# Sink attention: the low part of a weight tile is made one unit later, and the scalar engine's copies out of PSUM are moved ahead of the high part

## The reference, cut to what matters

```python
def attention_mixer(h, norm_w, w_in, q_norm_w, k_norm_w, sinks, w_out):
    u = rms_norm(h, norm_w) @ w_in
    q, k, v, gate = jnp.split(u, [...], axis=-1)
    q = rms_norm(q..., q_norm_w); k = rms_norm(k..., k_norm_w)
    o = banded_sink_attention(q, k, v, sinks)   # softmax over band, meta tokens and sink
    return (o * jax.nn.silu(gate)) @ w_out
```

## Time and profile before

| | us |
|---|---|
| times of three runs | 1647.33, 1652.02, 1652.57 |
| median | 1652.02 |
| span of the profiled execution, first to last instruction (no time of its own beside it) | 1649.1 |
| sink attention, first score matmul to first output matmul | 1150.7 to 1222.1 |
| TensorE busy | 1598.4 (97%) |
| VectorE busy | 1166.7 (71%) |
| ScalarE busy | 907.0 (55%) |
| DMA traffic | 230.02 MB, mean 139 GB/s |

### The profile page before, as it was taken

How to read it: one execution, slowest core, us unless ns; L and a number is a source line. 1 busy time by engine, 2 the same in 40 slices (tenths; PEclk the granted TensorE clock), 3 DMA queues, 4 the chain that set the end, 5 groups by cost and what they waited for, 6 DMA issues and landing times. The chain is left out here.

```text
span 1649.1 us, 33817 instructions
## 1 busy us (share of the span) xinstructions
PE 1598.4 (97%) x12970; PEld 1430.6 (87%) x12970; DVE 1166.7 (71%) x2011; ACT 907.0 (55%) x1622; POOL 74.0 (4%) x41
## 2 busy tenths in 40 slices
PE   7999999999999999999999999999899999999998
PEld 6888988999999999998888888887667889888877
DVE  5678666789888999986666666655765657655565
ACT  4347653454555767766666666653665644344443
POOL 0000000200000000000000000000001333200000
PEclk9989999999999999999999999999999999999999
DMA  6542355565554444446666666643123445300014
GB/s 225 189 134 86 117 158 167 166 183 169 184 178 144 140 139 131 139 140 207 191 192 192 192 196 194 191 134 103 52 77 93 151 152 155 122 10 3 3 35 145
DMA packets 63222, 230.02 MB, mean 139 GB/s; under 512 B 7024, under 2 KB 7280, under 8 KB 63104
## 3 DMA queue, kind: packets, MB, share of 16 engines
q1 hardware_dynamic: 63104, 228.37, 44.6%
HBM read 227.30 MB, written 1.05 MB: 138 GB/s over the span
## 5 line engine op out<-in xcount | busy, mean ns | idle before, releaser
L1141 DVE TENSOR_TENSOR tile_low<-weights,tile_high 128x1024 fp32r<-128x1024 f32 x252 | 307.9, 1222 | 141.3 <-ACT tile_high L1131 141.1
L1131 ACT ACTIVATE tile_high<-weights 128x1024 fp32r<-128x1024 f32 x252 | 268.1, 1064 | 134.0 <-issue 134.0
L183 ACT ACTIVATE tile_high<-weights 128x1024 fp32r<-128x1024 f32 x169 | 178.4, 1058 | 236.4 <-issue 61.9
L1213 PE MATMUL banks<-parts,tile_high 128*128 128x256 f32 x2048 | 272.0, 286 | 0.9 <-ACT tile_high L1131 0.6
L195 DVE TENSOR_TENSOR tile_low<-weights,tile_high 128x1024 fp32r<-128x1024 f32 x146 | 179.8, 1233 | 130.7 <-ACT tile_high L183 115.7
L1213 PEld LDWEIGHTS banks<-parts,tile_high 128*128 128x128 f32 x2048 | 255.5, 193 | 1.7 <-issue 1.7
L1533 PE MATMUL banks<-tile_high,parts 128*128 128x512 f32 x1024 | 253.0, 389 | 0.9 <-ACT parts L1491 0.9
L1533 PEld LDWEIGHTS banks<-tile_high,parts 128*128 128x128 f32 x1024 | 192.2, 188 | 40.9 <-issue 1.1
L237 PE MATMUL banks<-parts,tile_high 128*128 128x272 f32 (+1 forms) x1216 | 169.5, 293 | 0.0
L237 PEld LDWEIGHTS banks<-parts,tile_high 128*128 128x128 f32 x1216 | 158.1, 192 | 8.7 <-issue 7.5
L1218 PE MATMUL banks<-parts,tile_low 128*128 128x256 f32 x1024 | 144.3, 284 | 4.1 <-DVE tile_low L1141 4.0
(11 more groups left out here) (402 smaller groups left out, 2163.1 us busy)
## 6 DMA issues: line engine op xcount, KB each, us to landing
weights<-in_peer_u SPq DMA_DIRECT2D x128, 512.0 KB, 3.5
weights<-in_peer_v SPq DMA_DIRECT2D x128, 512.0 KB, 3.5
weights<-in_dn_in SPq DMA_DIRECT2D x49, 512.0 KB, 3.5
weights<-in_in_t SPq DMA_DIRECT2D x19, 512.0 KB, 3.6
weights<-in_attn_t SPq DMA_DIRECT2D x19, 512.0 KB, 3.6
weights<-in_in_m SPq DMA_DIRECT2D x16, 512.0 KB, 3.6
weights<-in_wq SPq DMA_DIRECT2D x16, 512.0 KB, 4.2
weights<-in_dn_out SPq DMA_DIRECT2D x16, 512.0 KB, 3.6
```

What stands on the lines that cost most here:

```text
L183: k.nc.scalar.activation(k.high[:, m % 2, :], k.ring.view(n), ACT.Copy).then_inc(*k.high_made.up())
L1131: k.nc.scalar.activation(k.high[:, (s + j) % 2, :], k.ring.buf[:, j % RING, :], ACT.Copy).then_inc(k.high_made.sem, 1)
L1141: k.nc.vector.tensor_tensor(k.low[:, (s + j) % 2, :], k.ring.buf[:, j % RING, :], k.high[:, (s + j) % 2, :].bitcast(F32), ALU.subtract).th ...
L1213: ins = nc.tensor.matmul(ps[:, bank, 0:S], high[:, c, :], x[:, c, :], start=part + c == 0, stop=False)
```

## The change

On DVE, `make_low` for the tile of an even unit moves from the end of that unit to the end of the next (odd) one. On ACT, `store` and `copy_turned` move ahead of `make_high` (and of `open_gates(0)` in the last turn) and of the gate copy. The amount of work is the same.

```diff
                 if u in meta_steps:
                     meta["vector"][meta_steps.index(u)](dve)
-                if u in ahead:
-                    make_low(dve, k, ahead[u])
+                if u - 1 in ahead:
+                    make_low(dve, k, ahead[u - 1])
...
                 if u < len(units):
                     exps(u)
+                if u >= 2:
+                    store(u - 2)
+                if 1 <= u <= len(units):
+                    copy_turned(u - 1)
                 if u == len(units):
                     open_gates(0)
                 elif u in ahead:
                     make_high(act, k, ahead[u])
                 if u and u % 2 == 0:
                     act.wait_ge(k.ring.used.sem, gate_tile(u // 2 - 1) + 1)
                     nc.scalar.activation(T[:, GATE + u // 2 - 1, :], fill, ACT.Copy).then_inc(*gated.up())
-                if u >= 2:
-                    store(u - 2)
-                if 1 <= u <= len(units):
-                    copy_turned(u - 1)
```

## The result

The changed kernel took 1669.02 us (median of 4 runs, 1665.58 to 1673.06) against 1651.04 us for the kernel before (4 runs), a ratio of 1.0115 with a 95% interval of 1.0098 to 1.0132. It is slower by 18 us. The forecast was 1665, from 1657.5 to 1671. The profiled execution of the changed kernel took 1665.58 us, with a span of 1663.8.

What follows compares the result with a forecast made beforehand. PE was taken as the bound, busy 63.29 of 71.37 us. Net stalls +7.0, last turn +1.9 and clock drops +4.2 gave +13.1 us on the 1652.0 median: 1665 us, range 1657.5 to 1671.

Steps and rivals of the forecast that it cites:

- `make_low` later removes the old gaps and costs nothing elsewhere: DVE's list: PE's waits for scale before turn, 4.6 us in seven units, can go; later low parts cost 0.
- The gate copy's stall: ACT's list, even units 2 to 14: PE waits 1.72 us for the late gate copy, 12.0 us in all.
- Old gaps vanish after the stall, net +7.0: PE in units 2 to 14: 5.0 us of old gaps go against 12.0 of stalls, net +7.0 us.
- The last turn, +1.9: Stage end: open_gates(0) behind copy_turned(15) puts the first output matmul 5.33 us after turn(15), not 3.46, +1.9 us.
- The clock, three drops of 1.4 = 4.2 us: PE's clock after the seven stalls: three falls to 0.50 at 1.4 us, 4.2 us; bounds 0 and 9.8.
- The count, two to five: PE's clock in the stage: two to five new stretches at 0.50; this forecast case had chance 0.55.
- the drop at the stage's end: First output matmuls: PE's clock falls to 0.50 there before and after, so no added cost was counted.
- nearly every stall: Rival, PE's clock: six or seven drops add 8.4 to 9.8 us, 1669 to 1671 us; chance 0.12.
- Mostly hidden: Rival: DVE sets the pace, each stall costs only 0.6 us, 4.2 in all, so 1656 us; chance 0.07.
- faster: Rival: part 1 saves 4.6 us, the ACT copies moved ahead cost nothing, 1647 us; chance 0.04.
- Clock stays up: Rival, PE's clock: at most one drop in seven gaps, +8.9 to 10.3, 1661 to 1662 us; chance 0.22.

Runs made afterwards that it cites:

- the last experiment: Kernel before with make_low one unit later, plus 4 filling matmuls ahead of values(15): 1644.81 us, ratio 0.9980.
- The stalls filled: Changed kernel plus 7 idle matmuls on PE in each of the seven gate-copy stalls: 1663.33 us, ratio 1.0088.
- DVE edit alone: Kernel before with only make_low moved to the odd unit, ACT's list as before: 1645.08 us, ratio 0.9976.
- the filled kernel: Changed kernel plus 7 idle matmuls per stall, 4 ahead of values(15) and 10 behind it: 1661.16 us, ratio 1.0073.
- the first execution: First profiled execution of the changed kernel, nothing further changed: 1665.58 us, turn 1 to 15 in 71.25 us.
- the second execution: Another profiled execution of the changed kernel, nothing further changed: turn 1 to 15 in 76.84 us.

## Why the prediction was right or wrong

- **`make_low` later removes the old gaps and costs nothing elsewhere: right.** Alone it made the kernel 4 us faster. Turn 1 to 15 fell from 59.13 to 55.53 us, although one step there (5-6, 5.14) holds a drop of the clock, and to 54.15 in the execution of the last experiment, which holds none; 4.6 us of gaps were forecast.
- **The gate copy's stall: right, mechanism and size.** Forecast 7 x 1.72 = 12.0 us, measured 11.8. The single stalls were 1.67 in four units, 1.33 and 1.45 in units 6 and 8, where the longer scores of tt = 1 already run ahead of the short copy of tt = 0, and 2.32 in unit 14. That one I had missed: no scores are left there to cover its first 0.66 us. The misses cancel but for 0.2 us, which is luck. That the gate copy's place is the cause is shown by putting it first: no stall, no loss.
- **Old gaps vanish after the stall, net +7.0: right.** The stalls filled, less one drop, gave +7.1.
- **The last turn, +1.9: right.** The output was forecast 5.33 us after `turn(15)` and came after 5.48, which is +2.0 on the 3.46 of the kernel before, and restoring only that turn took it back (to 2.86). The price is larger than it looks: the 3.46 hold values matmuls at the lower clock (1.53 us, 1.02 at full). At the full clock the same turn takes 2.96 (DVE edit alone) or 2.86, so the late Silu costs 2.5 to 2.6 us of waiting there. In the changed kernel the Silu starts 1.29 us after its table load, which is now exposed. The page "ScalarE: Activation LUTs" of the Trainium skill, section "What ACT_TABLE_LOAD costs", counts a drain of some 1.38 us on top. The trace doesn't show one: the load begins 0.02 us after the copy ahead of it ends (1231.97), so the measured step holds.
- **The clock, three drops of 1.4 = 4.2 us: too small.** This is the term that failed in size. The waits make 9.1 us of the 18 to 21 that the change cost, and the clock's part is 9 us by the filled kernel, more where that one kept a drop. The count, two to five, was right: three drops in the stage in the first execution, five in the second. Their price was not. Beyond the 66.2 us that turn 1 to 15 takes with the stalls alone, three drops cost 71.25 - 66.2 = 5.1 us and five cost 10.6, so 1.7 to 2.1 each. I had priced a drop by the one group of matmuls after it, but there are long stretches at the lower clock (0.57 mean over 12 us and twice over 8 us in the second execution) through which PE works on. And I wrote that the drop at the stage's end is there before and after: it is longer after, 5.02 and 5.28 us for the first output group against 3.96. Two gaps (1.09 and 2.54 us) stand there where one stood, but they don't settle it alone, since behind the same two gaps the group took 4.50 us with the gate copy put first. One of the drops, in unit 5 to 6, comes without any stall too. Without one it costs 1.5 us (5.14 against 3.64 us in an execution that holds no drop), with the stall 2.2 in the first execution and 3.7 in the second, over steps 5-6 and 6-7.
- **The forecast as a whole: the sum was 4.9 us short, the level 4.0.** Forecast +13.1, measured +18.0; the base of 1652.0 was 1 us above the kernel before as it was measured beside the changed one, and that hides a part of the miss. The median lies in the upper half of the range, where only the rival "nearly every stall" (1669 to 1671) stood. That rival had the time but not the count: three and five of seven stalls went with a drop. The Trainium skill ("TensorE: Matmul & The Clock Gate", section "A second HAM failure mode: psum-queue depth-cycling") tells of a kernel in which PE was idle for short spells between groups of matmuls often enough to make the clock swing. The traces here agree in part: the clock swings with stalls of 1.67 us and once with one of 0.72, and it stays up through four stalls of the first execution (1.45, 1.67, 1.67 and 2.32 us).
- **The rivals.** "Mostly hidden" and "faster" fall: the table's steps grow by the whole excess of the stall over the old gap. "Clock stays up" falls too, by the drops in the traces. The kernel with all gaps filled took 1661.16 us, which is that rival's number, but only because the rival counts from 1652.0 and the kernel before took 1647.54 beside this one: by its ratio it is +12.0, where the rival said +9.

## What to carry to other kernels

When a step is moved up in an engine's list, look at what is passed and who waits for that: here two copies were moved past a small one that freed a PSUM bank, and the busiest engine waited for the small one. A copy that frees the accumulator for the next product belongs ahead of everything that waits for a later product, and a change of two edits is best priced edit by edit, since here one was worth -4 us and the other +22 to +24. Where TensorE runs without pause, count short gaps twice, once as waiting and once as lost clock.

## What the runs showed of the hardware that was not expected

- The granted clock can fall to 0.50 where PE has no gap at all: it did so behind 32 matmuls of 16x16 in five profiled executions (0.50 from 1173.40 to 1176.70 us in that of the DVE edit alone), and at the same place in five more where a stall stands. With the recurring stalls of 0.72 us it fell once.
- Filling the gaps with matmuls that nothing reads gave back 9 us of 21, and the steps of units 9 to 14 stayed as they were (5.80 us) while the filling was no longer than the gap.
- The executions of one kernel differ by where and how often the clock falls: the kernel before ran from 1646.7 us at a mean clock of 0.997 to 1652.5 at 0.994, the changed kernel from 1665.6 to 1673.1 at 0.990 to 0.986. A difference of 2 or 3 us between single runs of such a kernel says nothing.
